# Strassen's scheme for 24 projection blocks of a three-block fp32 model, the sums on VectorE

## The chip, the cores and the metric

The kernel runs on one core of one Trainium2 chip. The metric is the device time of one execution in microseconds. Everything is fp32: a sequence of 512 tokens, model width 1024.

## The reference, cut to what matters

Three blocks follow each other on one activation matrix: a mixer of linear attention and sparse attention, a convolution and neighbourhood mixer with 16 experts, and two layers of a third kind. The change touches the projections of the third block and the store for weights of the experts.

```python
def even_layer(x, ...):
    proj = rms_norm_3(x, norm_g) @ w_in                # 1024 x 5632
    u_a, v_a, z_a, q_b, k_b, v_b, z_b = split_cols(proj, EVEN_SPLITS)
    a_out = chunked_sgu(u_a, v_a, ...) * silu(z_a)
    b_out = window_attention(q_b, k_b, v_b, sink) * silu(z_b)
    return concatenate([a_out, b_out]) @ w_out

def odd_layer(x, ...):
    proj = rms_norm_3(x, norm_g) @ w_in                # 1024 x 5 * 2048
    q, f_f, f_b, i, z = split_cols(proj, ODD_SPLITS)
    # f = lb + (1-lb) sigmoid(f_logit), k = 1-f, decays = exp(cumsum(log f)) in chunks of 64,
    # forward (f_f) and backward (f_b); o = both directions
    return (rms(o) * head_norm_g * silu(z)) @ w_out
```

## The kernel before, in words

Weights stream from HBM in blocks of 2 MB: 1024 rows by 512 columns, in SBUF as `w[128, 8, 512]`. `plan` lists them in the order of use, and `Chip.stream` issues their DMAs on SP's queue, each as soon as the slot it goes to is free (L202 to L212). Outside the experts four slots (`weight_ring`, `RING = 4`) turn over; in the experts stage eight do: the ring, three pairs of `work` slots and, last, `hT`.

`project` (L248) runs one list of tiles over the blocks. For a tile, TensorE accumulates one PSUM bank over eight 128-row pieces; a tile of kind "T" is 128 output columns by 512 tokens (L331), one of kind "N" has the tokens on the partitions (L335). Four tiles make a block. Tile n uses bank n mod R and waits until the eviction of tile n - R is done (R is 8 in the even layer's first projection, 4 in its second, 3 in the odd layer). ScalarE or VectorE evicts each tile in order of tiles. Behind tile n each engine runs whatever the dictionaries `tensor_beside`, `scalar_beside` and `vector_beside` hold for n; a key n - 0.5 is TensorE work in the middle of tile n. Each engine runs its part strictly in the written order, so a wait in it holds all that is behind it. A `project` is one block of the program, and the next starts when all engines have finished it.

The even layer (`even_layer`): six blocks (u, v, z, two each), then q, q and k/v with the gating (`even_gating`: layer norm on VectorE, a mix on TensorE that needs all of the norm, gates on VectorE) beside them, then the window attention.

The odd layer (`odd_group`) runs four head groups G. Each is one `project` with three banks: from the second group on eight tiles that add the group before to the residual (L2188), then the blocks F, B (forget gates of both directions), I, Q and Z, four tiles each, first tiles tF, tB, tI, tQ, tZ. Beside them: `log`, `scan`, `exponents`, `end_keys` for direction 0 during B and for direction 1 during I; `turn(d)` on TensorE needs `end_keys(d)`; `turn(1)` stands behind tile tI + 3; `products` and `step` run during Q, `gram`, `mask`, `output`, `norm_sum`, `root` and `finish` during Z.

`Norm` scales the activations into `hT` piece by piece on VectorE (L477, eight steps), once ScalarE has the reciprocal root; the first tile of a projection follows piece by piece.

Of the kernel before, what the change touches and what calls it, by code (L numbers as in the profile page):

```python
# [29 lines left out]
RING = 4  # L30
SLOT = 4096
# [79 lines left out]
class Chip:  # L111


    def __init__(self, nc, ctx, arrays, plan):
        self.nc, self.ctx, self.A, self.plan = nc, ctx, arrays, plan

        def sb(name, shape, dt=F32):
            return ctx.enter_context(nc.sbuf_tensor(name, shape, dt))

        self.xT = sb("xT", [P, KD, T])  # L120
        self.hT = sb("hT", [P, KD, T])
        self.ring = sb("weight_ring", [P, RING, SLOT])
# [12 lines left out]
        for n in ("tensor_step", "vector_step", "scalar_step", "pool_step", "aux_loaded", "tile_vector_done"):  # L135
# [6 lines left out]
        self.slot_of = [(i - first) % len(self.slots) if first <= i < first + 12 * E_ else i % RING  # L142
                        for i in range(len(plan))]
        self.arrived = {}
        self.issued = 0
        self.used = 0
# [66 lines left out]

    def block_view(self, i):
        _, kt, c = self.plan[i]
        return self.slots[self.slot_of[i]][:, 0:kt * c].rearrange("p (k c) -> p k c", k=kt)
# [29 lines left out]
def project(ch, nblocks, tiles, ahead=RING, extra_sync=None, vector_after=None, scalar_after=None,  # L246
# [19 lines left out]
    R = banks  # L266
    ready, by_act, by_dve = ch.counters("tile_ready", "tile_scalar_done", "tile_vector_done")
# [3 lines left out]
    def shape(t):  # L271
        b, kind, where, src, ntok, _ = t
        c = ch.plan[first + b][2] if b is not None else P
        if kind == "T":
            return min(P, c - where), ntok
        if kind == "N":
            return P, c
        if isinstance(kind, tuple):
            return P, kind[2] - kind[1]
        return P, P  # L280
# [5 lines left out]
    with nc.Block() as block:  # L286
# [7 lines left out]
        def _(pe):  # L294
            last = -1
            tensor_beside.get(-1, nothing)(pe)
            for n, t in enumerate(tiles):
# [21 lines left out]
                if kind == "M":  # L319
# [37 lines left out]
        @block.vector  # L357
        def _(dve):
            v = Line(dve, ch.S["vector_step"])
            if norm:  # L360
# [1362 lines left out]
def route(ch):  # L1723
# [80 lines left out]
def experts(ch):  # L1804
# [39 lines left out]
    with nc.Block() as block:  # L1844
        @block.sync
        def _(sp):
            ch.stream(sp, first + 12 * E_ + RING)
# [223 lines left out]
def even_gating(ch, beside, n0):  # L2071
# [18 lines left out]
    def layer_norm(line, dve):  # L2090
        for s in range(4):
# [4 lines left out]
        line.after(root, 1)  # L2096
        line(dve.reciprocal(mv[:, :, 1], mv[:, :, 1]))
        line.after(loaded, 16)
        for s in range(4):
            line(dve.tensor_scalar(v[:, s, :], v[:, s, :], mv[:, s, 0:1], mv[:, s, 1:2], SUB, MUL))  # L2100
            line(dve.tensor_tensor(v[:, s, :], v[:, s, :], gain, MUL))
            line(dve.tensor_tensor(v[:, s, :], v[:, s, :], shift, ADD), normed)

# [30 lines left out]
    beside.add(0, None, deviation, layer_norm)  # L2134
# [64 lines left out]

def even_layer(ch, norm):  # L2200
# [3 lines left out]
    for b in range(2):  # L2204
        tiles += [(b, "T", j * P, ch.hT, T, copy_to(u[:, 4 * b + j, :])) for j in range(4)]
    for b in range(2):
        tiles += [(2 + b, "N", s * P, ch.hT, T, copy_to(v[:, s, b * 512:(b + 1) * 512])) for s in range(4)]
    for b in range(2):
        tiles += [(4 + b, "T", j * P, ch.hT, T, act_to(z[:, 4 * b + j, :], ACT.Silu)) for j in range(4)]
    project(ch, 6, tiles, norm=norm)  # L2210
# [3 lines left out]
    for b in range(2):  # L2214
        tiles += [(b, "T", j * P, ch.hT, T, copy_to(q[:, 4 * b + j, :])) for j in range(4)]
# [3 lines left out]
    load = even_gating(ch, beside, 4)  # L2219
# [24 lines left out]
def odd_group(ch, G, norm):  # L2244
# [17 lines left out]
    by_dve, by_act = ch.S["tile_vector_done"], ch.S["tile_scalar_done"]  # L2262
    logged, scanned, decayed, ended = ch.counters("f_logged", "decay_scanned", "decay_exponents", "end_keys_ready")
# [8 lines left out]
    tF, tB, tI, tQ, tZ = [n0 + 4 * i for i in range(5)]  # L2272
    for d, dst in ((0, F), (1, B)):
        for j in range(4):
            lb = ch.sm[:, 16 * d + 4 * G + j:16 * d + 4 * G + j + 1]
            om = ch.sm[:, 32 + 16 * d + 4 * G + j:33 + 16 * d + 4 * G + j]

            def part_a(a, act, ps, sig, o=dst[:, j, :]):
                a(act.activation(o, ps, ACT.Sigmoid), sig)

            def part_v(v, dve, ps, sig, o=dst[:, j, :], k=kd[d][:, j, :], lb=lb, om=om):
                v(dve.tensor_scalar(o, o, om, lb, MUL, ADD))
                v(dve.tensor_scalar(k, o, -1.0, 1.0, MUL, ADD), sig)
            tiles.append((b0 + d, "T", j * P, ch.hT, T, (part_a, part_v)))
    tiles += [(b0 + 2, "N", s * P, ch.hT, T, copy_to(I[:, s, :])) for s in range(4)]
    for j in range(4):
        tmp = aT[j % 2].rearrange("p h v -> p (h v)")

        def q_a(a, act, ps, sig, j=j, tmp=tmp):
            if j >= 2:  # L2290
                a.after(by_dve, n0 + 7 + j)
# [6 lines left out]
    tiles += [(b0 + 4, "T", j * P, ch.hT, T, act_to(Z[:, j, :], ACT.Silu)) for j in range(4)]  # L2298

# [14 lines left out]
    def products(i):  # L2314
        def part(pe):
            for d in range(2):
                c = i if d == 0 else 7 - i
                s, rows = c // 2, slice(64 * (c % 2), 64 * (c % 2) + 64)
                if i == 0:
                    pe.wait_ge(natural.sem, natural.at(8))  # L2320
                else:
# [8 lines left out]
    def gram(h):  # L2330
        def part(pe):
            pe.wait_ge(by_dve.sem, by_dve.at(n0 + 9 + h))
# [43 lines left out]
    def log(d):  # L2376
        def part(a, act):
            a.after(by_dve, n0 + 4 * d + 4)
# [39 lines left out]
    def scan(d):  # L2418
        def part(v, dve):
            if d == 0:  # L2420
# [3 lines left out]
            for j in range(4):  # L2424
# [4 lines left out]
    def end_keys(d):  # L2429
        def part(v, dve):  # L2430
# [3 lines left out]
            v(dve.tensor_tensor(kd[d], kd[d], ed[d], MUL))  # L2434
            v(dve.tensor_tensor(ed[d].rearrange("p j (c t) -> p (j c) t", t=64),
# [31 lines left out]
    def finish(h):  # L2467
        def part(v, dve):
# [3 lines left out]
            v.after(by_act, 17 + h)  # L2472
            v(dve.scalar_tensor_tensor(Z[:, h, :], t, ch.v("hgrn_head_norm_g_3", 4 * G + h), Z[:, h, :], MUL, MUL))
        return part

    project(
        ch, b0 + 5, tiles, banks=3, norm=norm,
        tensor_beside={
            tI + 1: turn(0), tI + 3: turn(1), tQ: products(0), tQ + 0.5: products(1), tQ + 1: products(2),
            tQ + 1.5: products(3), tQ + 2: products(4), tQ + 2.5: products(5), tQ + 3: seq(products(6), gram(0)),  # L2480
            tZ - 0.5: gram(1), tZ: output(0), tZ + 0.5: seq(gram(2), output(1)), tZ + 1: seq(norm_sum(0), gram(3)),
            tZ + 1.5: seq(norm_sum(1), output(2)), tZ + 2: output(3), tZ + 2.5: seq(norm_sum(2), norm_sum(3))},
        scalar_beside={
            tB: log(0), tB + 2: exponents(0), tI: log(1), tI + 1: seq(exponents(1), to_natural(0)),
            tI + 3: to_natural(1), tZ: seq(square(0), square(1)), tZ + 1: seq(root(0), root(1), square(2)),
            tZ + 2: seq(square(3), last_roots)},
        vector_beside={
            tB + 1: scan(0), tB + 3: seq(end_keys(0), scan(1), end_keys(1)),
            tQ: seq(step(0), step(1)), tQ + 1: seq(step(2), step(3)), tQ + 2: seq(step(4), step(5)),
            tQ + 3: seq(step(6), *[mask(0), mask(1), mask(2), finish(0), mask(3), finish(1), finish(2), finish(3)])})  # L2490
# [116 lines left out]
```

## Time and profile before

| | us |
|---|---|
| median of 3 runs | 3687.27 (3686.51 to 3687.99) |
| profiled execution | 3687.83, of which the traced span 3686.1 |
| TensorE matmul busy | 3406.9 (92%) |
| TensorE weight load busy | 1654.7 (45%) |
| VectorE busy | 1217.0 (33%) |
| ScalarE busy | 733.1 (20%) |

Busy time of matmuls counts overlapped records once. A matmul of fp32 shows as two matmul records and two weight loads, so a tile of eight pieces has 16 of each. TensorE's granted clock is 0.967 of full speed over the span.

### The profile page before, as it was taken

The page shows a single profiled execution, that of the slowest core. Times are in us where ns is not written, and L with a number is a line of the kernel's source. Part 1 is how long each engine was busy: PE and PEld are TensorE (multiplying, and loading weights), DVE is VectorE, ACT ScalarE, POOL GpSimd, SP SyncE. Part 2 cuts the span into 40 slices and gives each one's busy share as a digit, 9 for nine tenths or more (in the row PEclk, how much of TensorE's full clock was granted, in tenths as well). Part 3 has the DMA queues.
Part 4 walks back from the last instruction along what each step waited for, and adds up shares of the span by engine and source line. Part 5 has one row for each costly group of instructions (what it writes and reads, how often), then busy time and mean ns, then how long its engine had stood idle before and what let it go on. Part 6 is the DMA issues. An engine that isn't in the chain of part 4 may idle for free. (4 is left out here: it accounts for less than half of the span.)

```text
span 3686.1 us, 36428 instructions
## 1 busy us (share of the span) xinstructions
PE 3406.9 (92%) x15170; PEld 1654.7 (45%) x15170; DVE 1217.0 (33%) x1973; ACT 733.1 (20%) x1128; POOL 0.2 (0%) x4
## 2 busy tenths in 40 slices
PE   7998998998999969989999987999999999999997
PEld 3485544443446533323233232445543544546454
DVE  3562238511466232221212212013432414233242
ACT  2110222302015220000000002011512223232223
POOL 0000000000000000000000000000000000000000
PEclk9997999999999979999999999999999999999999
DMA  7201042123110059999999998222111111111100
GB/s 261 78 3 69 23 154 104 46 89 129 69 61 26 23 210 428 428 427 428 428 428 427 428 427 341 69 86 73 46 69 46 69 46 69 46 69 46 69 23 23
DMA packets 120292, 588.13 MB, mean 160 GB/s; under 512 B 8896, under 2 KB 11072, under 8 KB 95424
## 3 DMA queue, kind: packets, MB, share of 16 engines
q1 hardware_dynamic: 120128, 585.80, 39.9%
q8 instruction: 121, 1.98, 0.2%
q14 instruction: 43, 0.35, 0.0%
HBM read 583.68 MB, written 2.10 MB: 159 GB/s over the span
## 5 line engine op out<-in xcount | busy, mean ns | idle before, releaser
L331 PE MATMUL ps<-hT,weight_ring 128*128 128x512 f32 x2624 | 1166.8, 601 | 42.8 <-DVE hT L477 13.4
L331 PEld LDWEIGHTS ps<-hT,weight_ring 128*128 128x128 f32 x2624 | 496.8, 192 | 645.2 <-issue 628.4
L331 PE MATMUL ps<-work,weight_ring 128*128 128x512 f32 (+1 forms) x960 | 425.1, 596 | 30.9 <-PEq L286 24.4
L331 PEld LDWEIGHTS ps<-work,weight_ring 128*128 128x128 f32 x960 | 184.0, 196 | 242.0 <-issue 233.6
L1891 PE MATMUL ps<-weight_ring,work 128*64 128x512 f32 x1024 | 236.0, 605 | 33.5 <-DMA weight_ring<-in_w_up 23.6
L335 PE MATMUL ps<-weight_ring,hT 128*128 128x512 f32 (+2 forms) x640 | 248.7, 544 | 0.0
L1891 PE MATMUL ps<-work 128*64 128x512 f32 x768 | 174.8, 597 | 23.6 <-DMA work<-in_w_up 12.4
L335 PEld LDWEIGHTS ps<-weight_ring,hT 128*128 128x128 f32 x640 | 117.7, 194 | 120.8 <-issue 118.8
L2020 DVE SCALAR_TENSOR_TENSOR xT<-ps,mod,xT 128x512 f32<-128x512 f32 x128 | 96.2, 751 | 226.4 <-PE ps L1909 224.0
L420 ACT COPY work<-ps 128x512 f32<-128x512 f32 (+1 forms) x85 | 48.2, 567 | 581.1 <-PE ps L335 290.9
L1891 PEld LDWEIGHTS ps<-weight_ring,work 128*64 128x64 f32 x1024 | 71.4, 138 | 189.9 <-issue 135.7
L1270 PE MATMUL ps<-work 64*128 64x256 f32 (+5 forms) x256 | 106.2, 522 | 20.1 <-DVE work L1314 13.1
L1945 PE MATMUL ps<-weight_ring,work 128*64 128x512 f32 x512 | 113.9, 596 | 2.6 <-issue 2.3
L1891 PEld LDWEIGHTS ps<-work 128*64 128x64 f32 x768 | 53.7, 136 | 137.3 <-issue 107.4
L2188 DVE TENSOR_TENSOR xT<-ps,xT 128x512 f32<-128x512 f32 x48 | 33.2, 692 | 202.6 <-PE ps L331 202.6
L1296 PE MATMUL ps<-work 128*64 128x128 f32 (+1 forms) x704 | 99.8, 285 | 0.0
L2015 DVE TENSOR_TENSOR work<-work,ps 128x512 f32<-128x512 f32 x32 | 33.9, 1059 | 196.7 <-PE ps L1891 196.1
L1971 ACT ACTIVATE work<-ps 128x512 f32<-128x512 f32 x32 | 19.1, 597 | 385.5 <-PE ps L1891 385.0
L2035 DVE COPY work<-ps 128x512 f32<-128x512 f32 x16 | 11.1, 692 | 244.3 <-PE ps L1945 244.3
L1580 DVE SCALAR_TENSOR_TENSOR work<-work,vectors 128x512 f32<-128x512 f32 x120 | 90.2, 752 | 4.3
L1945 PE MATMUL ps<-work 128*64 128x512 f32 x384 | 85.9, 596 | 3.5 <-issue 2.3
L1296 PEld LDWEIGHTS ps<-work 128*64 128x64 f32 (+1 forms) x704 | 81.6, 153 | 11.2 <-issue 10.2
(311 smaller groups left out, 3152.0 us busy)
## 6 DMA issues: line engine op xcount, KB each, us to landing
weight_ring<-in_w_gate SPq DMA_DIRECT2D x32, 2048.0 KB, 35.4
weight_ring<-in_w_down SPq DMA_DIRECT2D x32, 2048.0 KB, 35.4
weight_ring<-in_w_up SPq DMA_DIRECT2D x32, 2048.0 KB, 33.3
work<-in_w_up SPq DMA_DIRECT2D x24, 2048.0 KB, 32.0
work<-in_w_gate SPq DMA_DIRECT2D x24, 2048.0 KB, 35.4
work<-in_w_down SPq DMA_DIRECT2D x24, 2048.0 KB, 35.4
weight_ring<-in_w_in_odd SPq DMA_DIRECT2D x20, 2048.0 KB, 7.8
weight_ring<-in_w_in SPq DMA_DIRECT2D x18, 2048.0 KB, 9.0
```

The lines of the kernel that those rows point to most:

```text
L331: ins = pe.matmul(bank[0:m, 0:f], w[:, k, where:where + m], src[:, k, 0:ntok], start=k == 0, stop=k == kt - 1)
L335: ins = pe.matmul(bank[0:m, 0:f], src[:, k, where:where + P], w[:, k, c0:c0 + f], start=k == 0, stop=k == kt - 1)
L420: return (lambda a, act, ps, sig: a(act.copy(out, ps), sig), None)
L1270: ins = pe.matmul(self.score_banks(i)[:, c0:c0 + n], u["q"], k, start=True, stop=True)
L1296: ins = pe.matmul(self.ch.ps[u["rows"], self.value_bank + gi % 2, u["col"]:u["col"] + P], val, self.pT[(i - 3) % 2][:, t * P:(t + 1) * P], ...
L1580: v(dve.scalar_tensor_tensor(y[:, j, :], src, tap, y[:, j, :], MUL, ADD))
L1891: ins = pe.matmul(ps[64 * h:64 * h + 64, 1 + 2 * u + n, :], xs[:, 2 * (i % 2) + t, i // 2, :], w[:, t, c0:c0 + 512], start=i == 0 and t == ...
L1945: ins = pe.matmul(ps[64 * q:64 * q + 64, 7, :], hidT[:, i // 2, t, i % 2, :], w[:, t, q * 512:(q + 1) * 512], start=i == 0 and t == 0, sto ...
L1971: a(act.activation(sil[:, p, :], ps[:, 1 + p, :], ACT.Silu), silus)
L2015: v(dve.tensor_tensor(by_tile(hid[:, p, :]), strided(sil[:, p, :]), strided(ps[:, 3 + p, :]), MUL), hid_ready)
L2020: v(dve.scalar_tensor_tensor(ch.xT[:, n, :], ps[:, scatter_banks(e, i // 2)[i % 2], :], ch.mod2[:, 40 + n, 0:1], ch.xT[:, n, :], MUL, ADD) ...
L2188: v(dve.tensor_tensor(ch.xT[:, n, :], ps, ch.xT[:, n, :], ADD), sig)
```

## The change

A projection block of 1024 x 512 weights times 1024 x 512 activations is cut into halves on each side. Instead of four tiles (eight pieces of 512 columns each) it is computed as seven products of half size (Strassen's scheme in Winograd's form): each product is a tile of eight matmuls of 256 columns, two column halves of four pieces, in one bank. Four sums of weight quarters (`weight_sum`, 4 x 256 elements per partition each) and, once for each layer, four sums of activation quarters (`activation_sums`, the same size) are made on VectorE. The seven products are evicted by one ScalarE copy and seven VectorE additions of 128 x 512. This is done for u, v, z (six blocks) and q (two) of the even layer, and for F, B, I and Z of the four odd groups (sixteen). The sums of the next block stand behind early tiles of the current one; the first block of each layer has its sums ahead of the norm's scaling (`vector_first`), and the activation sums stand behind it.

What an eviction did on the way (sigmoid and the bounds for F and B, silu for z) is now done by quarters after the last addition to the quarter. In the odd layer the side work is spread anew over 7 tiles; `gated` is split from `finish`, `inner_keys` from `end_keys`. The third block's ring has three slots, since the fourth holds the activation sums; a new tensor `spare_slot` holds two or three of the weight sums there and is a ninth slot for weights in the experts stage, ahead of `hT` in the turn.

```diff
+RING3 = 3
+        self.spare = sb("spare_slot", [P, SLOT])
+        self.slots.insert(-1, self.spare[:, :])
+        self.slot_of = [i % RING if i < first else (i - first) % len(self.slots) if i < last else (i - last) % RING3
+                        for i in range(len(plan))]
...
+PRODUCTS = (1, 6, 7, 5, 3, 4, 2)
+def weight_sum(ch, i, n):
+        out, x, y, op = ((s1, a21, a22, ADD), (s2, s1, a11, SUB), (s3, a11, a21, SUB), (s4, a12, s2, SUB))[n]
+        v(dve.tensor_tensor(out, x, y, op), ch.S["weight_sums"])
+def activation_sums(ch):
+        for out, x, y in ((t1, b12, b11), (t2, b22, t1), (t3, b22, b12), (t4, t2, b21)):
+            v(dve.tensor_tensor(out, x, y, SUB), ch.S["h_sums"])
+    evictions = {1: (first, None), 6: (None, add((d12, d11, ADD), after_copy=True)), 7: (None, add((d21, d12, ADD))),
+                 5: (None, add((d22, d21, ADD), (d12, d12, ADD))), 3: (None, add((d12, d12, ADD))),
+                 4: (None, add((d21, d21, SUB))), 2: (None, add((d11, d11, ADD)))}
+    return {1: (a11, b11, 0, 0), 2: (a12, b21, 0, 0), 3: (s4, b22, 4, 0), 4: (a22, t4, 0, 4), 5: (s1, t1, 1, 1),
+            6: (s2, t2, 2, 2), 7: (s3, t3, 3, 3)}[p]
...
+                    for j in range(2):
+                        for k in range(4):
+                            ins = pe.matmul(bank[:, j * L:(j + 1) * L], st, mv, start=k == 0, stop=k == 3)
...
-            ch.stream(sp, ch.used + RING + 3)
+            ch.stream(sp, ch.used + RING + 4)
             sp.wait_ge(turned.sem, turned.at(9))
-            ch.stream(sp, ch.used + RING + 4)
+            ch.stream(sp, ch.used + RING + 5)
...
+    for s in range(4):
+        beside.add(s // 2, vector=variances(s))
+        beside.add(3 + 2 * s, vector=layer_norm(s))
+    load = even_gating(ch, beside, 10)
...
+    scalar = {
+        tB + 0: log(0), tB + 2: exponents(0), tI: log(1), tI + 2: seq(exponents(1), to_natural(0)),
+        tI + 5: to_natural(1), tZ + 1: square(0), tZ + 2: square(1), tZ + 3: root(0), tZ + 4: seq(root(1), square(2))}
+    vector = {
+        tB: bounded(0, (0, 1), 4), tB + 1: scan(0, (0, 1)), tB + 2: scan(0, (2, 3)), tB + 4: inner_keys(0),
+        tB + 5: end_keys(0), tI: bounded(1, (0, 1), 4), tI + 1: scan(1, (0, 1)), tI + 2: scan(1, (2, 3)),
+        tI + 3: inner_keys(1), tI + 4: end_keys(1), ...
+        tZ + 4: finish(1), tZ + 6: seq(gated(0), gated(1), finish(2), gated(2), finish(3), gated(3))}
+        tI + 2: turn(0), tI + 5: turn(1), ...
+        beside.add(t + 6, vector=bounded(d, (2, 3), 3))
+    for n, quarter in quarters_done(0):
+        beside.add(tZ + max(n, 5), scalar=open_gate(quarter, n))
+    beside.add(tZ + 6, scalar=last_roots)
+        beside.add(tB + 1 + n, vector=weight_sum(ch, first + 2, n))
+        beside.add(tI + min(4 + n, 6), vector=weight_sum(ch, first + 4, n))
```

## Rows read from the trace of the kernel before

**Rows 1.** Busy time by stretch; length, busy PE, PEld, DVE, ACT, POOL, clock, DMA
```profile
2304.00:2469.00 165.00, 164.68 (x381) 72.99 (x382) 5.44 (x8) 14.85 (x24) 0.00 (x0) 0.99 0.19 64
2981.60:3197.00 215.40, 209.76 (x745) 111.62 (x744) 70.77 (x94) 56.23 (x63) 0.00 (x0) 0.99 0.17 59
```
**Rows 2.** Timeline of TensorE in the even layer; columns: start, length, what
```profile
2507.26 7.03 PE L331 MATMUL ps<-hT,weight_ring 128*128 128x512 f32 x16
2514.12 1.05 PE L2116 MATMUL ps<-work 128*128 128x128 f32 x8
...
2546.05 3.62 PE L335 MATMUL ps<-weight_ring,hT 128*128 128x256 f32 x16
2549.51 1.05 PE L2116 MATMUL ps<-work 128*128 128x128 f32 x8
```
**Rows 3.** Weight loads grouped by line, even layer; busy, mean ns | idle before
```profile
L335 PEld LDWEIGHTS ps<-weight_ring,hT 128*128 128x128 f32 x64 | 11.9, 190 | 1.5
```
**Rows 4.** VectorE groups by line and shape, even layer and odd layer
```profile
L2093 DVE BATCH_NORM_STATS2 small<-work 128x6 f32<-128x512 f32 x8 | 5.6, 694 | 162.5 <-PEq L286 162.3
...
L2101 DVE TENSOR_TENSOR work<-work 128x1024 f32<-128x1024 f32 x4 | 4.9, 1226 | 0.1
...
L2100 DVE TENSOR_SCALAR work<-work,small 128x1024 f32<-128x1024 f32 x4 | 3.2, 812 | 1.1 <-DMA work<-in_gmlp 1.0
...
L2426 DVE TENSOR_TENSOR_SCAN work<-work 128x512 f32<-128x512 f32 x32 | 39.2, 1224 | 11.0 <-ACT work L2380 9.7 <-DVE work L2422 0.3
L2188 DVE TENSOR_TENSOR xT<-ps,xT 128x512 f32<-128x512 f32 x37 | 25.6, 692 | 142.4 <-PE ps L331 142.4
L2435 DVE TENSOR_TENSOR work<-work,small 128x2048 f32<-128x2048 f32 x8 | 18.3, 2292 | 0.3
L2282 DVE TENSOR_SCALAR work<-work,small 128x512 f32<-128x512 f32 x32 | 17.5, 546 | 172.3 <-ACT work L2279 172.2
...
L2283 DVE TENSOR_SCALAR work<-work 128x512 f32<-128x512 f32 x32 | 13.7, 427 | 1.1
```
**Rows 5.** Timeline of ScalarE: an activation of 2048 elements in an odd group
```profile
3079.86 1.91 ACT L2380 ACTIVATE work<-work 128x2048 f32<-128x2048 f32 x1
```
**Rows 6.** Timeline of TensorE, I block to Q block of that group
```profile
3084.58 1.91 PE L2308 MATMUL ps<-masks,work 128*128 128x128 f32 x16
3086.33 13.90 PE L335 MATMUL ps<-weight_ring,hT 128*128 128x512 f32 x32
```
**Rows 7.** Timeline from the end of one odd group to the next: TensorE, ScalarE, VectorE
```profile
3193.46 3.60 PE L331 MATMUL ps<-hT,weight_ring 128*128 128x512 f32 x8
3202.30 30.70 PE L331 MATMUL ps<-work,weight_ring 128*128 128x512 f32 x64 [5.25 <-PEq L286]
...
3193.70 1.28 ACT L2413 ACT_TABLE_LOAD   x1 [4.59 <-PE ps L2371]
...
3201.02 0.75 DVE L2473 SCALAR_TENSOR_TENSOR work<-work,vectors 128x512 f32<-128x512 f32 x1 [0.37 <-ACT work L424]
```
**Rows 8.** Busy time by stretch behind that gap (columns as in rows 1)
```profile
3204.00:3209.00 5.00, 5.00 (x8) 2.05 (x7) 0.00 (x0) 0.00 (x0) 0.00 (x0) 0.57 0.01 4
```
**Rows 9.** Timeline at the start of the even layer: ScalarE, VectorE, TensorE
```profile
2299.47 1.28 ACT L429 ACT_TABLE_LOAD   x1 [2.98 <-PEq L488]
...
2303.43 6.26 DVE L477 SCALAR_TENSOR_TENSOR hT<-xT,vectors,work 128x512 f32<-128x512 f32 x8 [8.12 <-ACT work L430]
...
2312.95 0.59 ACT L420 COPY work<-ps 128x512 f32<-128x512 f32 x1 [9.56 <-PE ps L331]
```
**Rows 10.** Busy time by stretch around the start of the experts and inside them
```profile
1350.00:1355.00 5.00, 3.13 (x14) 1.06 (x12) 2.04 (x5) 0.59 (x1) 0.00 (x0) 0.84 0.00 0
...
1600.00:1650.00 50.00, 46.37 (x210) 15.68 (x212) 11.74 (x19) 3.54 (x6) 0.00 (x0) 1.00 1.01 429
```
**Rows 11.** Timeline of SP's DMA issues: the first after the pause
```profile
1360.23 10.63 SPq L207 DMA_DIRECT2D weight_ring<-in_w_down  x4
```
**Rows 12.** Waits of TensorE from 1540 to 2300 us
```profile
PE ps L1891 <- DMA weight_ring<-in_w_up: 22.9, 25, 2.2
```

More of the change, by code:

```diff
@@ L266, in project @@
     R = banks
+    if ahead is None:
+        ahead = RING3 if first >= min(ch.sum_order) else RING
+    weight_ready, h_ready = ch.S["weight_sums"], ch.S["h_sums"]
     ready, by_act, by_dve = ch.counters("tile_ready", "tile_scalar_done", "tile_vector_done")
@@ L2088, in load, with variances, part @@
         loaded.total += 16
-    def layer_norm(line, dve):
-        for s in range(4):
+    def variances(s):
+        def part(line, dve):
             for i in range(2):
@@ L2095, in layer_norm, with part @@
                  var_ready if s == 3 else None)
[L2096 to L2099, printed above, removed]
+        return part
+    def layer_norm(s):
+        def part(line, dve):
+            if s == 0:
+                line.after(root, 1)
+                line(dve.reciprocal(mv[:, :, 1], mv[:, :, 1]))
+                line.after(loaded, 16)
             line(dve.tensor_scalar(v[:, s, :], v[:, s, :], mv[:, s, 0:1], mv[:, s, 1:2], SUB, MUL))
@@ L2197, in add_to_stream, with quarters_done, silu_quarter, part @@
     return norm
+def quarters_done(b):
+    return [(3, 3), (4, 1), (5, 2), (6, 0)]
+def silu_quarter(ch, x, done):
+    by_dve = ch.S["tile_vector_done"]
+    def part(a, act):
+        a.after(by_dve, done)
+        a(act.activation(x, x, ACT.Silu))
+    return part
 def even_layer(ch, norm):
@@ L2214, in even_layer @@
     for b in range(2):
-        tiles += [(b, "T", j * P, ch.hT, T, copy_to(q[:, 4 * b + j, :])) for j in range(4)]
+        seven_tiles(ch, tiles, b, False, quarters(q[:, 4 * b:4 * b + 4, :]))
     tiles += [(2, "T", j * P, ch.hT, T, copy_to(kv[:, j, :])) for j in range(2)]
@@ L2218, in even_layer @@
     beside = Beside()
[L2219 removed]
+    for n in range(4):
+        beside.add(1 + n, vector=weight_sum(ch, ch.used + 1, n))
+    load = even_gating(ch, beside, 10)
     beside.project(ch, 3, tiles, banks=4, extra_sync=load)
@@ L2271, in odd_group, with gates, part, bounded @@
     b0 = 1 if G else 0
[L2272 to L2281, printed above, removed]
-                v(dve.tensor_scalar(o, o, om, lb, MUL, ADD))
-                v(dve.tensor_scalar(k, o, -1.0, 1.0, MUL, ADD), sig)
-            tiles.append((b0 + d, "T", j * P, ch.hT, T, (part_a, part_v)))
-    tiles += [(b0 + 2, "N", s * P, ch.hT, T, copy_to(I[:, s, :])) for s in range(4)]
+    tF, tB, tI, tQ, tZ = n0, n0 + 7, n0 + 14, n0 + 21, n0 + 25
+    first = ch.used + b0
+    seven_tiles(ch, tiles, b0, False, quarters(F))
+    seven_tiles(ch, tiles, b0 + 1, False, quarters(B))
+    seven_tiles(ch, tiles, b0 + 2, True, quarters(I, True))
+    def gates(d, quarter, done):
+        def part(a, act):
+            x = quarters((F, B)[d])[quarter]
+            a.after(by_dve, n0 + 6 * d + done)
+            a(act.activation(x, x, ACT.Sigmoid), sigmoids)
+        return part
+    def bounded(d, rows, need):
+        def part(v, dve):
+            v.after(sigmoids, 4 * d + need)
+            for j in rows:
+                o, k = (F, B)[d][:, j, :], kd[d][:, j, :]
+                lb = ch.sm[:, 16 * d + 4 * G + j:16 * d + 4 * G + j + 1]
+                om = ch.sm[:, 32 + 16 * d + 4 * G + j:33 + 16 * d + 4 * G + j]
+                v(dve.tensor_scalar(o, o, om, lb, MUL, ADD))
+                v(dve.tensor_scalar(k, o, -1.0, 1.0, MUL, ADD), bounds)
+        return part
+    def open_gate(quarter, done):
+        def part(a, act):
+            x = quarters(Z)[quarter]
+            a.after(by_dve, n0 + 22 + done)
+            a(act.activation(x, x, ACT.Silu), gate_open)
+        return part
     for j in range(4):
@@ L2297, in odd_group @@
         tiles.append((b0 + 3, "T", j * P, ch.hT, T, (q_a, q_v)))
-    tiles += [(b0 + 4, "T", j * P, ch.hT, T, act_to(Z[:, j, :], ACT.Silu)) for j in range(4)]
+    seven_tiles(ch, tiles, b0 + 4, False, quarters(Z))
     def turn(d):
@@ L2423, in part @@
             v.after(logged, d + 1)
-            for j in range(4):
+            for j in rows:
                 x = F[:, j, :] if d == 0 else B[:, j, ::-1]
@@ new lines, in odd_group @@
+    for k, part in vector.items():
+        beside.add(k, vector=part)
+    for n in range(4):
+        if G:
+            beside.add(1 + n, vector=weight_sum(ch, first, n))
+        beside.add(tF + 1 + n, vector=weight_sum(ch, first + 1, n))
+        beside.add(tB + 1 + n, vector=weight_sum(ch, first + 2, n))
+        beside.add(tI + min(4 + n, 6), vector=weight_sum(ch, first + 4, n))
+    if norm:
+        ch.counter("h_sums")
+        beside.add(-1, vector=activation_sums(ch))
+    beside.project(ch, b0 + 5, tiles, banks=3, norm=norm, vector_first=weight_sums(ch, first) if norm else None)
```

157 lines of the change are left out of this document (119 added, 38 removed).

## The prediction, made before the change was run

> **What bounds the kernel now.** I read the page's busy shares first, then the busy time by stretch. TensorE is the bound: in the even layer's first projection it is busy 164.7 of 165.0 us, in an odd group 209.8 of 215.4, while VectorE works 5.4 and 70.8 us there [rows 1]. So a shorter TensorE stream pays at once, as long as VectorE keeps up. The exception is the experts stage: there the DMA engines are full at 429 GB/s and TensorE waits for weights in short pieces [rows 10, 12]. Third, I read the timelines of all engines through one odd group, because each engine runs in a written order and the chain logarithm, scan, exponents, keys, turn goes back and forth between them [rows 5, 6]. Last come the seams between program blocks, where TensorE is idle for 5.25 us [rows 7].
>
> **TensorE's work.** A tile of 16 records of 512 columns takes 2514.12 - 2507.26 = 6.86 us, one of 16 records of 256 columns 2549.51 - 2546.05 = 3.46 us [rows 2]: 429 and 216 ns a record. A block was 4 x 6.86 = 27.44 us and becomes 7 x 3.46 = 24.22. That is 3.22 us less, for 24 blocks **-77.3 us**. The doubled number of weight loads is hidden in that row: a load takes 190 ns [rows 3] and fits into the 216 ns pitch, with 26 ns to spare.
>
> Here a rule speaks against the change. The row shows loads on the same rows of the array as the running matmul, and a pitch no longer than the columns need. The Trainium skill, TensorE: Matmul & The Clock Gate, section "The mechanism", says that weight loads overlap with matmuls in flight only when the row group differs. By that rule a 256-column record would take 216 + 190 = 406 ns, a block 112 x 0.406 = 45.5 us; it is the last rival below. The pitch in rows 2 contradicts it.
>
> **VectorE's work for a block.** Four weight sums of 1024 elements at 1.226 us, seven PSUM additions at 0.692 us [rows 4], each with some 0.03 us between: 4 x 1.26 + 7 x 0.73 = 10.1 us against 24.2 of TensorE. In the even layer's first projection nothing else is there, and with eight banks it costs nothing. If that cover were gone, a block would wait up to 10 us.
>
> **Start of each layer (twice).** Before, VectorE began to scale at 2303.43, 4.0 us after ScalarE began the root [rows 9]. Four weight sums in front take 5.0 us: +1.0. Then the second product needs two activation sums behind all eight scalings: 6.26 + 2 x 1.26 = 8.8 us after the first scaling, while the first product (3.46, partly at the half clock) is done by about 6.2. Six products follow: the block ends 8.9 + 20.8 = 29.7 us after scaling began. Before, the first tile's eviction began 9.5 us after it [rows 9], so the tile ended at about 9.25, the block at 9.25 + 20.6 = 29.85. With the 1.0 the block is 0.85 later, where 3.22 earlier was booked: +4.1 each, **+8.2**.
>
> **Seam and gating in the even layer.** The last quarter's silu now follows a VectorE addition: +0.9. In the second projection VectorE has, up to the mix behind the eleventh tile, four variances (two statistics of 0.69 and an end of 0.2 each, 6.8 in all), 5.0 of sums, four norms of 0.81 + 2 x 1.23 (3.35 with gaps) and the additions [rows 4]; in the written order it is done at 38.9 us, TensorE is there at 38.1. +0.8. Together **+1.7**. These have one answer each within a microsecond.
>
> **An odd group, B and I.** I set VectorE's order against TensorE's tiles, time 0 at the end of F's last tile; an eviction can begin 0.27 us after a tile. The durations are those of the rows [rows 4, 5, 7]: 0.73 an addition, 1.04 a row of bounds (0.55 and 0.43 and their gaps), 1.25 a scan row, 1.26 a weight sum, 2.55 inner keys (a small copy and 2.29), 2.33 end keys, logarithm 1.28 (table) + 1.91, exponents 1.28 + 2 x 1.91 = 5.15.
> F's last addition ends at 1.0, its bounds at 3.1 and 5.2, the logarithm at 8.4. Then VectorE is full: ones for the scan and half of it to 11.1, sum 12.3, addition 13.1, scan 15.6, sum, two additions, sum, addition to 20.3; the exponents are there at 20.8; inner keys to 23.4, sum 24.6, addition 25.3, end keys 27.7, B's last addition 28.4 (its tile ended at 24.2: VectorE is 4 us late). B's bounds follow to 32.6, the logarithm to 35.8, scan, addition, scan to 41.6, exponents to 46.8, inner keys 49.4, addition 50.1, end keys **52.5**. TensorE reaches `turn(1)` after six I tiles and `turn(0)` (1.75, from 3084.58 to 3086.33 [rows 6]) at 24.2 + 20.8 + 1.75 = 46.7. So it waits 5.8 us where it had not waited: behind it on TensorE stand the last I product and all of Q. Four groups: **+23.2**. No tile waits for a bank: the nearest is tI + 1, which needs B's sixth addition at 25.3 and starts at 27.7.
>
> **The clock behind that wait.** After 5.25 us idle the granted clock was 0.57 in the stretch 3204 to 3209, and 64 records took 30.7 us instead of 64 x 0.429 = 27.5 [rows 7, 8]: 3.2 us lost. Bounds for a wait of 5.8 us: 0 and 3.2; I take 2.2, near the row, since the idle time is nearly the same, and below it, since this is the dearest of the three such seams. **+8.8**.
>
> **Q and Z.** Q is unchanged. In Z the same side work stands between seven shorter tiles; the nearest wait in my order is `output(2)` at 32.8 against `finish(0)` at 31.6: nothing. The end is new. Before, the roots of the last two heads ran during the last tile (from 3193.7) and the next group began 0.5 us after the last product of VectorE [rows 7]. Now they stand behind the last quarter's silu: addition to 0.9 us after the last tile, silu 1.5, two table loads and the first three activations 6.2, then VectorE's finish and gate for two heads, 4 x 0.74 = 3.0, and 0.5 for the seam: 9.7 us instead of 5.25. **+17.8** for four groups. The clock was low there already.
>
> **Experts.** DMA stands still at 1350 to 1355 since all slots are full [rows 10]; it goes on at 1360.23 with the first slot freed, and from there to the end of the experts it is the bound [rows 10 to 12]. With a ninth slot one more block of 2 MB is loaded in the pause, 2.1 MB / 0.427 = 4.9 us less to load afterwards: **-4.9**. Bounds: 0 if the last weights come as before, -4.9 if they come first. The shorter ring costs nothing: a load is due every 24 us and a transfer at full rate takes 4.9.
>
> **The sum.** -77.3 + 8.2 + 1.7 + 23.2 + 8.8 + 17.8 - 4.9 = -22.5 us. Made against the profiled execution (3687.83, 1.7 around its span), which lies 0.6 above the median of 3687.27: **3665**.
>
> **Rivals.**
> A. VectorE is not that late in I, or the clock stays up. My chain has some forty steps, and rows show each alone, not in this order. Without wait and clock loss it is -54.5 us, 3633; with half of both 3649. For it: VectorE is free for 6 of 24 us in F, and small gains at the start pass through. Against it: each duration is a row.
> B. VectorE is later than that. Three banks of half-size tiles give 10.4 us from a product to the need of its bank, where before it was 20.6. The margin is 2.4 us at tI + 1. If additions or sums on strided quarters took 10% longer, the two chains through B and I would end some 4 us later: 4 x 4 = +16, 3681; with a further bank wait it comes to no change.
> C. The ninth slot brings nothing (it does not do what it says): 3670.
> D. Slower than before: weight loads do not stay hidden when they fill 190 of 216 ns for a whole layer, with all other engines reading SBUF. The change has 24 x 112 = 2688 such records. The gain of 22.5 us is gone from 8.4 ns more a record (224 ns), and the kernel is slower by 0.2% from 227 ns. At 235 ns it is +29 us, 3716. Against it: 64 records of this shape keep to 216 ns in rows 2 and 3.
> E. The skill's rule on row groups holds: 24 x (45.5 - 27.4) is 434 us, 4120.
>
> **How the numbers follow.** The forecast has 0.48 (its own range 3655 to 3674, from the bounds of the clock and 1 us on each wait), A 0.20, B 0.20, C 0.05, D 0.06, E 0.01. The range is 3644 to 3683: it leaves out the far part of A (0.08), D, E, and the tail of B (0.03). About 0.2%, 7 us, is what a measurement of this kernel can tell from no change. Faster: 0.48 + 0.20 + 0.05 + 0.12 of B = 0.85. Same: 0.05 of B, 0.01 of D. Slower: 0.05 of D, 0.01 of E, 0.03 of B.
>
> **What would show it.** Right: 256-column records at 216 ns; TensorE idle some 6 us in each group until VectorE's end keys; the seam between groups at 9 to 10 us; a group still 213 to 217 us long, so that the odd layer gains almost nothing and the even layer 20 us; DMA still busy in 1330 to 1345. Wrong: no idle time ahead of the second turn (A), TensorE waiting for additions at its banks (B), a record above 220 ns (D).

## The result, and the profile after

The changed kernel takes 3668.4 us (median of 4 runs, 3666.4 to 3670.8) against 3687.6 of the kernel before on the same chip: a recorded ratio of 0.9944 with a 95% interval of 0.9931 to 0.9956 (the two medians alone give 0.9948). The profiled execution took 3666.36 us, which is 21.5 less than the profiled one of before; its span is 3664.5. The page's busy times, in us, with share and number of instructions:

```profile
PE 3336.9 (91%) x16322; PEld 1885.2 (51%) x16322; DVE 1459.9 (40%) x2245; ACT 714.9 (20%) x1104; POOL 0.2 (0%) x4
```

TensorE has lost 70 us of busy time, but the kernel only 21.5. The waits of TensorE from 2200 us on show the first part of the answer (who waited for whom: us in total, times, longest):

```profile
PE ps L452 <- PEq L392: 42.2, 6, 9.8
PE ps L2479 <- DVE work L2611: 23.9, 4, 6.0
PE ps L439 <- DVE hT L600: 15.6, 2, 9.4
...
PE ps L439 <- DVE weight_ring L292: 3.3, 2, 2.0
```

L2479 is `turn`, which waits for the end keys (L2611) four times for 6 us, where before it did not wait at all. The first line is the seams (PEq is TensorE's own sequencer, which starts the next block of the program): four of the six are 9.8 us, where rows 7 show 5.25.

One odd group on TensorE's timeline (start, length, what, idle before and its releaser), from the last I products to the next group:

```profile
2841.33 1.91 PE L2479 MATMUL ps<-masks,work 128*128 128x128 f32 x16
2843.08 3.62 PE L439 MATMUL ps<-spare_slot,weight_ring 128*128 128x256 f32 x16
2846.53 3.62 PE L439 MATMUL ps<-spare_slot,hT 128*128 128x256 f32 x16
2849.99 3.62 PE L439 MATMUL ps<-weight_ring 128*128 128x256 f32 x16
2859.57 3.58 PE L2479 MATMUL ps<-masks,work 128*128 128x128 f32 x16 [5.96 <-DVE work L2611]
2862.98 3.62 PE L439 MATMUL ps<-weight_ring,hT 128*128 128x256 f32 x16
...
2956.48 1.89 PE L439 MATMUL ps<-hT,weight_ring 128*128 128x256 f32 x8
2968.18 29.67 PE L452 MATMUL ps<-work,weight_ring 128*128 128x512 f32 x64 [9.81 <-PEq L392]
...
3183.21 29.67 PE L452 MATMUL ps<-work,weight_ring 128*128 128x512 f32 x64 [9.79 <-PEq L392]
```

Products start 3.45 us apart: 16 records of 256 columns at 216 ns, as in rows 2. `turn(0)` takes 1.75 us to the next start, `turn(1)` behind the wait 3.41: it ran at the lower clock. A whole group, from the first of the tiles that add a group's share to the residual (L452, `work`) to the next such tile, takes 3183.21 - 2968.18 = 215.03 us, where it took 215.41 (from 2986.89 to 3202.30, rows 7). Four of five blocks are cheaper by 27.44 - 24.17 = 3.27 us each there, and the group is 0.4 us shorter.

VectorE in the same stretch shows where the end keys come from, and that it is not simply full (lines in order of time):

```profile
2838.50 0.55 DVE L2448 TENSOR_SCALAR work<-work,small 128x512 f32<-128x512 f32 x1
2839.08 0.43 DVE L2449 TENSOR_SCALAR work<-work 128x512 f32<-128x512 f32 x1
2839.55 0.69 DVE L324 TENSOR_TENSOR work<-work,ps 128x512 f32<-128x512 f32 x1
2842.90 2.48 DVE L2598 TENSOR_TENSOR_SCAN work<-work 128x512 f32<-128x512 f32 x2 [2.67 <-ACT work L2552]
2845.42 0.69 DVE L324 TENSOR_TENSOR work<-work,ps 128x512 f32<-128x512 f32 x1
2846.14 2.48 DVE L2598 TENSOR_TENSOR_SCAN work<-work 128x512 f32<-128x512 f32 x2
2848.65 1.41 DVE L324 TENSOR_TENSOR work<-work,ps 128x512 f32<-128x512 f32 x2
2853.94 0.20 DVE L2604 COPY small<-work 128x32 f32<-128x32 f32 x1 [3.88 <-ACT work L2560]
2854.17 2.29 DVE L2606 TENSOR_TENSOR work<-work 128x2048 f32<-128x2048 f32 x1
2856.50 0.69 DVE L324 TENSOR_TENSOR work<-work,ps 128x512 f32<-128x512 f32 x1
2857.22 2.29 DVE L2611 TENSOR_TENSOR work<-work,small 128x2048 f32<-128x2048 f32 x1
```

Twice it waits for ScalarE (2.67 us for the logarithm, 3.88 for the exponents) while the chain goes through there.

The experts: the first slot is freed at 1358.90 (SP's next issue), and the last expert's scatter starts at 2267.86, which is 908.96 us later. Before these were 1360.23 [rows 11] and 2273.79: 913.56. The ninth slot brought 4.6 us, and the slot freed 1.3 us sooner the rest of the 5.9 us by which the scatter starts earlier.

### The profile page after: what moved, and what is told of

Read it like the earlier page. It is cut to its first block and busy times, and to the rows that moved or that the text cites. A ratio compares the mean times of both kernels' runs of the same rounds, so it can differ in the third digit from the quotient of the medians.

```text
span 3664.5 us, 39233 instructions
## 1 busy us (share of the span) xinstructions
PE 3336.9 (91%) x16322; PEld 1885.2 (51%) x16322; DVE 1459.9 (40%) x2245; ACT 714.9 (20%) x1104; POOL 0.2 (0%) x4
## 5 line engine op out<-in xcount | busy, mean ns | idle before, releaser
L452 PE MATMUL ps<-hT,weight_ring 128*128 128x512 f32 x1472 | 663.0, 606 | 28.2 <-ACT hT L591 8.8
L452 PE MATMUL ps<-work,weight_ring 128*128 128x512 f32 (+1 forms) x960 | 425.3, 596 | 49.2 <-PEq L392 42.6
L452 PEld LDWEIGHTS ps<-hT,weight_ring 128*128 128x128 f32 x1472 | 279.9, 194 | 368.6 <-issue 354.0
L452 PEld LDWEIGHTS ps<-work,weight_ring 128*128 128x128 f32 x960 | 184.4, 196 | 259.0 <-issue 250.6
L2014 PE MATMUL ps<-weight_ring,work 128*64 128x512 f32 x944 | 214.3, 597 | 32.8 <-DMA weight_ring<-in_w_up 18.7
L324 DVE TENSOR_TENSOR work<-work,ps 128x512 f32<-128x512 f32 x168 | 115.5, 687 | 272.9 <-PE ps L439 270.3
L2014 PE MATMUL ps<-work 128*64 128x512 f32 x688 | 156.5, 597 | 21.4 <-DMA work<-in_w_up 13.3
L439 PE MATMUL ps<-weight_ring 128*128 128x256 f32 x768 | 174.0, 380 | 0.0
L439 PEld LDWEIGHTS ps<-weight_ring 128*128 128x128 f32 x768 | 145.2, 190 | 19.4
L439 PE MATMUL ps<-hT,weight_ring 128*128 128x256 f32 x576 | 137.2, 394 | 17.6 <-DVE hT L600 15.6
L439 PE MATMUL ps<-weight_ring,spare_slot 128*128 128x256 f32 x576 | 132.3, 383 | 3.3 <-DVE weight_ring L292 3.3
L439 PEld LDWEIGHTS ps<-hT,weight_ring 128*128 128x128 f32 x576 | 113.2, 198 | 39.1 <-issue 22.9
L439 PEld LDWEIGHTS ps<-weight_ring,spare_slot 128*128 128x128 f32 x576 | 109.8, 192 | 19.0 <-issue 4.1
L2138 DVE TENSOR_TENSOR work<-work,ps 128x512 f32<-128x512 f32 x32 | 33.9, 1060 | 192.0 <-PE ps L2014 191.4
L2068 PE MATMUL ps<-weight_ring,work 128*64 128x512 f32 x448 | 100.2, 595 | 4.0 <-DMA weight_ring<-in_w_down 2.4
```

Source lines behind the costliest of these rows:

```text
L324: v(dve.tensor_tensor(out, x, got, op), sig if out is steps[-1][0] else None)
L439: ins = pe.matmul(bank[:, j * L:(j + 1) * L], st, mv, start=k == 0, stop=k == 3)
L452: ins = pe.matmul(bank[0:m, 0:f], w[:, k, where:where + m], src[:, k, 0:ntok], start=k == 0, stop=k == kt - 1)
L2014: ins = pe.matmul(ps[64 * h:64 * h + 64, 1 + 2 * u + n, :], xs[:, 2 * (i % 2) + t, i // 2, :], w[:, t, c0:c0 + 512], start=i == 0 and t == ...
L2068: ins = pe.matmul(ps[64 * q:64 * q + 64, 7, :], hidT[:, i // 2, t, i % 2, :], w[:, t, q * 512:(q + 1) * 512], start=i == 0 and t == 0, sto ...
L2138: v(dve.tensor_tensor(by_tile(hid[:, p, :]), strided(sil[:, p, :]), strided(ps[:, 3 + p, :]), MUL), hid_ready)
```

## The experiments

Executions differ upstream of the change: in the kernels with nine slots the first slot is freed between 1356.3 and 1363.9 us, with the same code up to there. On the second chip the kernel before spread from 3679 to 3695 us. So beside each time I give one distance in the trace, **D**: from the start of the last expert's scatter to the start of the first tile behind the last odd group. TensorE's rows for it, first of the kernel before, then of the changed one:

```profile
2273.79 3.95 PE L1909 MATMUL ps<-work 64*128 64x512 f32 x16 [0.86 <-DVE work L2035]
...
3635.20 8.70 PE L331 MATMUL ps<-work,weight_ring 128*128 128x512 f32 x16 [5.22 <-PEq L286]
```

```profile
2267.86 3.95 PE L2032 MATMUL ps<-work 64*128 64x512 f32 x16 [0.86 <-DVE work L2158]
...
3613.31 9.06 PE L452 MATMUL ps<-work,weight_ring 128*128 128x512 f32 x16 [9.81 <-PEq L392]
```

It is 1361.4 us before and 1345.5 in the changed kernel. Each D is read from one execution, and it too moves by 2 to 3 us with the clock between executions of the same code (the run with eight slots shows it), so a difference of D is safe only where the places that moved are named.

### Which part brings what

**Only the slots.** Both layers as before; ninth slot and ring of three kept.

```diff
# in short: these functions are exchanged whole
-def even_gating, even_layer, odd_group   # of the changed kernel
+def even_gating, even_layer, odd_group   # of the kernel before
```

> Even and odd layer as before (four tiles a block, no sums); of the change only the ninth slot in the experts stage and the ring of three stay. Theory (the ninth slot is worth 4.9 us, the shorter ring nothing): 3681.6 us against 3686.5 of before, and the last expert's scatter begins 909 us after the first slot is freed instead of 913.6. Rival (the ring of three costs something in the third block): above 3684 us, with waits of TensorE for weights of the third block. The distance from here to the run with only the odd layer as before is the worth of the eight even blocks; by the terms of the sum it is 77.3 / 3 = 25.8 less 4.1, 1.7 and two clock losses of 1.8 each, 16 us.

Measured: 3685.3 us against 3688.3 in the same session (ratio 0.9990, 0.9979 to 1.0). The scatter begins 2265.08 - 1356.27 = 908.8 us after the first free slot, 4.8 less than before, and D is 1361.7. The ninth slot brings its 4.8 us. The shorter ring costs nothing that shows in the third block: D is within 0.3 us of before, and TensorE has no wait for weights there. The median shows 3.0 us less, which this spread (3678.6 to 3688.9 in ten executions) can't tell from 4.8; by the time alone (above 3684) the rival would have looked right.

**Eight slots.** The changed kernel without the ninth.

```diff
-        self.slots.insert(-1, self.spare[:, :])
...
-            ch.stream(sp, ch.used + RING + 4)
+            ch.stream(sp, ch.used + RING + 3)
...
-            ch.stream(sp, ch.used + RING + 5)
+            ch.stream(sp, ch.used + RING + 4)
```

> The changed kernel with eight slots in the experts stage as before (spare_slot holds only weight sums). Theory (the DMA-bound stage begins with one block more to load, 2.1 MB at 427 GB/s): 4.9 us slower than the changed kernel, 3673. Rival (the 6.3 us between the two traces were all the ninth slot): 6 us or more slower. Second rival (nothing: another limit ends the stage): within 1 us.

Measured: 3669.9 us, only 1.5 above the changed kernel. The experts do take 2273.21 - 1359.04 = 914.2 us instead of 909.0, 5.2 more. Half of it came back behind them: D is 3616.20 - 2273.21 = 1343.0, 2.5 less than in the changed kernel, though this part of the code is the same. Three tiles behind short idle times ran at the full clock in this execution and at the lower one in the changed kernel, 1.7 us each: two behind seams, and the second product of the odd layer. About half of that was lost again, where other tiles (the first turn above all, 2.8 us lost for 1.7) stayed at the lower clock for longer. By the time alone this would have been a miss for the ninth slot.

**The odd layer as before**, even layer changed.

```diff
# in short: this function is exchanged whole
-def odd_group   # of the changed kernel
+def odd_group   # of the kernel before
```

> The changed kernel with the whole odd layer as before (four tiles a block, no sums), the even layer and the ninth slot as changed. Theory (16 of the 24 blocks bring nothing, since the wait, the clock and the longer seam take what the products save): from the first odd matmul to the last group's end 836.5 us instead of 837.0, and 1 us less at its start: 3666 us, within 3 us of the changed kernel. Rival (the products in the odd layer bring a part, the gain in the even layer is smaller than read): 5 us or more slower than the changed kernel.

Measured: 3665.2 us, D = 3611.43 - 2265.74 = 1345.7. Against the run with only the slots (1361.7) the eight even blocks bring 16.0 us, as worked out. Of the two clock losses of 1.8 us in that working one stands at a seam with 2.06 us of idle time that the kernel before has too; it ran at the lower clock here and at the full one in the run with only the slots, so that this loss is luck, and without it the even blocks bring some 17.7 us. Against the changed kernel (1345.5) the **sixteen odd blocks bring 0.2 us**. In this pair both seams of the even layer ran at the same clock. The 0.2 stands for nothing measurable, not for a gain: the medians, 3665.2 and 3668.4 from different sessions, even put the kernel with the odd layer as before ahead.

### What eats the odd layer's products

**`turn(1)` later.**

```diff
-        tI + 2: turn(0), tI + 5: turn(1), tQ: products(0), ...
+        tI + 2: turn(0), tQ - 0.5: turn(1), tQ: products(0), ...
```

> The changed kernel with one move: turn(1) on TensorE stands in the middle of the first Q tile instead of behind the sixth I product. Theory (TensorE waits 5.96 us in each odd group for VectorE's end keys and then runs 1.7 us slower at the lower clock): both go, the seventh I product and half a Q tile (3.45 + 3.43 us) lie in front of the wait, 4 x 7.6 = 30 us less, 3638 us against 3668. Rival A (the wait only moves: products(0) behind the Q tile then waits for the copies of the turned keys): TensorE shows a new wait of 3 to 6 us at L2497 and the gain is under 15 us. Rival B (the clock loss is not from this wait): the wait goes, 24 us less, and some record group still shows the half clock.

Measured: 3638.8 us (ratio to before 0.9871, 0.9857 to 0.9886), D = 1316.6, that is 28.8 less than the changed kernel. TensorE's timeline:

```profile
2855.80 3.62 PE L439 MATMUL ps<-weight_ring,hT 128*128 128x256 f32 x16
2859.70 3.67 PE L452 MATMUL ps<-hT,weight_ring 128*128 128x512 f32 x8 [0.28 <-DVE work L324]
2863.21 1.91 PE L2479 MATMUL ps<-masks,work 128*128 128x128 f32 x16
2864.95 3.60 PE L452 MATMUL ps<-hT,weight_ring 128*128 128x512 f32 x8
2868.48 1.71 PE L2497 MATMUL ps<-work 64*128 64x128 f32 x16
```

`turn(1)` doesn't wait and takes 1.74 us; the copies of the turned keys are done when `products(0)` (L2497) comes, so rival A falls. A bank wait of 0.28 us is new. Both losses, the wait and the clock behind it, came from this one place; the four groups bring 28.8 / 4 = 7.2 us each, where 7.6 was worked out.

**Small sums beside B.** What is the wait made of? This kernel leaves out nearly all of block I's four weight sums (it sums one column in 256), so its block I is not the true one.

```diff
+        if small:
+            out, x, y = out[:, :, 0:1], x[:, :, 0:1], y[:, :, 0:1]
...
-        beside.add(tB + 1 + n, vector=weight_sum(ch, first + 2, n))
+        beside.add(tB + 1 + n, vector=weight_sum(ch, first + 2, n, small=True))
```

> Leaves out most of the four weight sums of block I beside block B (one column in 256 is summed, the instruction stays), so block I's products are not the true ones. It tells what the wait at turn(1) is made of. Theory (a serial chain of ScalarE and VectorE that is longer than seven... six short tiles, with VectorE's load only part of it): worked out with VectorE free of 4 x 1.1 us in B, the end keys come at 49.7 instead of 52.5 us after F's end, so the wait falls from 5.96 to about 3.0 us, not to 0. Rival (VectorE's load in B is all of it): the wait falls below 1.5 us. Second rival (load plays no part): it stays at 5.5 to 6 us.

Measured, in a single execution: 3667.5 us. The wait fell from 5.96 to 3.86 us:

```profile
2847.46 3.62 PE L441 MATMUL ps<-spare_slot,weight_ring 128*128 128x256 f32 x16
2850.92 3.62 PE L441 MATMUL ps<-spare_slot,hT 128*128 128x256 f32 x16
2854.37 3.62 PE L441 MATMUL ps<-weight_ring 128*128 128x256 f32 x16
2861.84 3.67 PE L2481 MATMUL ps<-masks,work 128*128 128x128 f32 x16 [3.86 <-DVE work L2613]
2865.31 4.59 PE L441 MATMUL ps<-weight_ring,hT 128*128 128x256 f32 x16
2869.74 0.59 PE L454 MATMUL ps<-hT,weight_ring 128*128 128x512 f32 x1
```

Both rivals fall: a third of the wait is the load of these sums on VectorE. Two thirds are left without it: the serial chain through two engines, with the other work of VectorE that stands in it, is still longer than six half-size tiles. The keys came 50.6 us after F's end where I had worked out 49.7; I did not follow these 0.9 us up. The time hides the gain, since the first slot was freed 5.0 us later here than in the changed kernel: D is 3614.57 - 2272.87 = 1341.7, 3.8 us less, where the four waits together are 8.5 shorter (15.4 for 23.9). The rest went to the clock. In the group shown the turn took 3.47 us to the next start and the product behind it 4.43 instead of 3.45, so that 2.7 us were lost instead of 1.7. It is not shown that the shorter wait caused this: over its four groups this run lost 2.7, 3.0, 3.0 and 1.4 us behind 3.86 us of idle time, and the run with eight slots, with the full wait of 5.96, lost 2.8, 1.9, 1.7 and 1.7.

**Z with four tiles**, on top of the late turn.

```diff
-    seven_tiles(ch, tiles, b0 + 4, False, quarters(Z))
+    tiles += [(b0 + 4, "T", j * P, ch.hT, T, act_to(Z[:, j, :], ACT.Silu)) for j in range(4)]
...
-        tZ + 4: seq(norm_sum(1), output(2)), tZ + 5: output(3), tZ + 5.5: seq(norm_sum(2), norm_sum(3))}
+        tZ + 1.5: seq(norm_sum(1), output(2)), tZ + 2: output(3), tZ + 2.5: seq(norm_sum(2), norm_sum(3))}
```

> The kernel with turn(1) moved into the first Q tile, and in it block Z of the odd groups as before (four tiles, silu at the eviction, roots under the last tile). Theory (Z's seven products give 3.3 us a group and take 4.6 at the seam): 4 x 1.3 = 5 us faster than with seven products, 3634 us, seam 5.25 us instead of 9.8. Rival (the longer seam is hidden or has another cause): slower by 13 us, 3652.

Measured: 3630.0 us, 8.8 less than with seven products; D = 1308.6, 8.1 less. The seam is back at 5.24 us:

```profile
2955.41 30.25 PE L452 MATMUL ps<-work,weight_ring 128*128 128x512 f32 x64 [5.24 <-PEq L392]
```

So in this order Z's seven products cost more than they gave. Of the 8.1 us 5.2 are the price that I worked out, 4 x (9.81 - 5.24 - 3.27). Another 1.7 and 1.6 are luck of the clock: the seam with 2.05 us of idle time and the second product of the odd layer ran at the full clock in this execution, and at the lower one in that of the late turn alone. The seams between groups lost 0.5 more.

### A better order

**Start and seam of the even layer**, on top of the late turn (Z with seven products).

```diff
-    beside.add(-1, vector=activation_sums(ch))
+    beside.add(-1, vector=first_sums(ch, first))    # T1, T2, S3, T3, S4, T4
...
-    vector_first=weight_sums(ch, first)
+    vector_first=early_sums(ch, first)              # S1, S2
...
-            for n, quarter in quarters_done(b):
+            for n, quarter in quarters_done(b)[:4 if b == 4 else 3]:
...
+    beside.add(0, scalar=lambda a, act: a(act.activation(rest, rest, ACT.Silu)))
```

> The kernel with turn(1) moved, and two more moves: only two of the four weight sums stand in front of the norm's scaling at a layer's start, the other two behind it in turn with the activation sums; and the last silu of z (even layer) stands behind the seam. Theory: the start of scaling comes 1.0 us earlier in both layers, the seam is 0.65 shorter (1.98 to 1.3 us idle), and the first product behind it runs at the full clock, 1.7: 1.0 + 1.0 + 0.65 + 1.7 = 4.4 us faster than with turn(1) alone, 3634. Rival (the low clock behind a short idle time does not hang on its length): 2.6 us faster or less, and the first product still takes 5.2 us.

Measured: 3632.8 us, 6.0 less than with the late turn alone; D = 1310.0, 6.6 less.

```profile
2451.54 3.69 PE L446 MATMUL ps<-hT,weight_ring 128*128 128x256 f32 x16 [1.32 <-PEq L399]
```

The seam is 1.32 us, and the product behind it runs at the full clock (5.38 before the move). It did so in both runs with this seam; with the longer one (1.98 us) it did in one run of six. Worked out were 4.4 us. By the luck told below 1.7 more came at the next seam and 1.6 at the second product of the odd layer; 0.7 was lost at the seams between the groups, and waits for banks took 0.3 more.

**Z's side work one product earlier**, on top of that.

```diff
-        tZ: gram(1), tZ + 1: output(0), tZ + 2: seq(gram(2), output(1)), tZ + 3: seq(norm_sum(0), gram(3)),
-        tZ + 4: seq(norm_sum(1), output(2)), tZ + 5: output(3), tZ + 5.5: seq(norm_sum(2), norm_sum(3))}
+        tZ: gram(1), tZ + 1: output(0), tZ + 2: seq(norm_sum(0), gram(2), output(1)),
+        tZ + 3: seq(norm_sum(1), gram(3), output(2)), tZ + 4: output(3), tZ + 5: seq(norm_sum(2), norm_sum(3))}
...
+    beside.add(tZ + 5, scalar=last_roots)
+    beside.add(tZ + 6, scalar=open_gate(*quarters_done(0)[3][::-1]))
```

> The kernel of the run before, and in block Z the norm sums, outputs and roots stand one product earlier; the roots of the last two heads on ScalarE stand ahead of the last quarter's silu instead of behind it. Theory (the seam is the chain norm sum, four table loads and activations, finish and gate, of which one product of 3.45 us more now covers a part): the seam falls from 9.8 to about 7.4 us, 4 x 2.4 = 10 us faster, 3624. Rival (the earlier order makes TensorE wait for roots or masks inside Z): new waits of TensorE at the outputs, as long or longer than what the seam gains.

Measured: **3619.0 us** (ratio to before 0.9807, 0.9788 to 0.9825), D = 1296.8.

```profile
2940.64 1.88 PE L2552 MATMUL ps<-work,masks 128*128 128x512 f32 x4
2942.36 3.62 PE L446 MATMUL ps<-hT,weight_ring 128*128 128x256 f32 x16
2952.45 17.77 PE L459 MATMUL ps<-work,weight_ring 128*128 128x512 f32 x37 [6.48 <-PEq L399]
```

A whole product lies between the last norm sums (L2552) and the seam, where it was half of one, and the seam falls to 6.48 us; four times 3.3 us is the gain of 13. The half product is 1.7 of the 3.3; ScalarE's roots ahead of the last silu were changed in the same run, and the two were not tried apart. Worked out were 2.4 us a seam, so the size was a miss. No new wait stands in Z. With this order Z's seven products are worth having: a group gains 3.27 us by them and its seam is 6.48 - 5.24 = 1.24 longer than with four tiles, which makes 8 us for four groups. The whole D is 11.8 us below that with four tiles; the rest is the moves at the starts and the even seam (4.3) and the clock, for and against. (Four tiles with the new order of Z were not tried.) This kernel beats both, with every product of the change kept.

## Why the prediction came out right, point by point

- **The sum.** Forecast -22.5 us against the profiled execution; measured -21.5. The likeliest case held, and no rival: `turn(1)` waits (against A), no bank wait in B and I (B), the ninth slot loads one block more in the pause (C), the products at the full clock keep to 216 ns a record (D, E). So the rule of the Trainium skill, TensorE: Matmul & The Clock Gate, section "The mechanism", that weight loads overlap with matmuls in flight only when the row group differs, does not hold for these matmuls: by it the starts would be 6.5 us apart, an estimate from rows 2 and 3 (16 x 0.406), and they are 3.45.
- **TensorE's work.** Forecast 24.22 us a block, measured 7 x 3.453 = 24.17: -78.5 instead of -77.3.
- **Start of each layer.** The even one came to the tenth: scaling begins at 2299.53, the block ends at 2329.25, 29.7 us later. In the odd one the second product, behind 2.02 us of idle time, ran at the lower clock, which the sum did not have. VectorE and TensorE there:

```profile
2775.38 6.26 DVE L600 SCALAR_TENSOR_TENSOR hT<-xT,vectors,work 128x512 f32<-128x512 f32 x8
...
2776.28 6.01 PE L439 MATMUL ps<-hT,weight_ring 128*128 128x256 f32 x16 [9.37 <-DVE hT L600]
2784.32 5.38 PE L439 MATMUL ps<-weight_ring,spare_slot 128*128 128x256 f32 x16 [2.02 <-DVE weight_ring L292]
2789.53 3.62 PE L439 MATMUL ps<-weight_ring 128*128 128x256 f32 x16
```

  The second product takes 5.21 us to the next start instead of 3.45: +1.8. The clock had come back before it and fell again: the granted clock in the middle and at the end of the first product, and in the second (columns as in rows 1):

```profile
2780.00:2781.00 1.00, 1.00 (x4) 0.82 (x3) 0.93 (x3) 0.00 (x0) 0.00 (x0) 0.50 0.00 0
2781.00:2782.30 1.30, 1.30 (x6) 0.78 (x5) 1.26 (x2) 0.00 (x0) 0.00 (x0) 1.00 0.00 0
...
2784.00:2789.50 5.50, 5.18 (x16) 4.29 (x17) 2.62 (x3) 0.00 (x0) 0.00 (x0) 0.69 0.00 0
```

- **Seam and gating.** Forecast +0.9 and +0.8; measured 1.98 - 1.16 = 0.8 and a wait of 0.9 at the mix. Missed: the product behind the seam ran at the lower clock.

```profile
2452.26 5.38 PE L439 MATMUL ps<-hT,weight_ring 128*128 128x256 f32 x16 [1.98 <-PEq L392]
2457.48 3.62 PE L439 MATMUL ps<-weight_ring,spare_slot 128*128 128x256 f32 x16
```

  The term was right in its place and 1.8 us too small. With it, and with the luck taken out, the even blocks bring 17.7 us and not the 20 that the prediction gives as a sign.
- **The wait at `turn(1)`.** Forecast 5.8, measured 5.96. What made this work was to write VectorE's order out against TensorE's tiles; busy shares (VectorE at 40%) show nothing of it.
- **The clock behind it.** Forecast 2.2, measured 3.41 - 1.75 = 1.7 in each of four groups of this execution. It is no fixed price: the run with eight slots, the same code here, lost 1.7 to 2.8.
- **The odd seam.** Forecast 9.7, measured 9.8.
- **Experts.** Forecast -4.9, measured -4.6 to -5.2 in three pairs of traces. The first slot was freed 1.3 us earlier beside, which is luck: with the same code up to there it is freed up to 3.7 us later than in the kernel before and up to 4.0 us earlier.

The misses (1.8 + 1.8 at short idle times, against 2.1 too much at the long waits, 1.2 in the products and 1.3 of luck) nearly cancel: by them alone it would be -23.5. Of the 2.0 us left, 0.9 is the clock behind an idle time of 5.77 us ahead of the even layer, which is there before too (1.9 us lost for 1.0), and the rest some tenths each in the wait (+0.6), the odd seam (+0.4) and the experts (+0.3). That the total came within 1 us is luck, since the clock alone moves it by 2 to 3; that it came near is not, as each of the dear terms (products, wait, odd seam, experts) is within some 6% of its size, the clock apart.

## What to carry to other kernels

When tiles get shorter, every chain that was hidden behind a fixed number of tiles must be measured again in microseconds: here six tiles of 3.45 us and a turn no longer cover a chain of 28 us through two other engines, and one tile no longer covers the roots at the end. Write the order of the second busiest engine out against the tiles before the change, as its mean load hides the wait; and if a wait appears, move the consumer before you lighten the producer: one moved key was worth 29 us, leaving out a block's sums on VectorE, a third of the wait, 4 us. A part of a change can be worth nothing in one order (sixteen blocks, 0.2 us) and some 45 us in another: D is 1345.7 with the odd layer as before and 1296.8 with the last order, of which 3.4 us belong to the moves in the even layer.

## What the runs showed of the hardware

A short idle time costs TensorE its clock in one execution and not in another, with the same code and the same idle time. Behind the even seam the changed kernel idled 1.98 us and its first product took 5.22 us to the next start. In the run with eight slots the idle time is the same and the product takes 3.5:

```profile
2458.09 3.69 PE L438 MATMUL ps<-hT,weight_ring 128*128 128x256 f32 x16 [1.98 <-PEq L391]
```

At the next seam 2.06 us of idle time are followed by 15.67 us for 32 records in the kernel before and in the changed one, and by 13.97 in four of the runs. The granted clock of the changed kernel ahead of the even seam and behind it (stretch, length, busy time of PE, PEld, DVE, ACT and POOL, clock, DMA):

```profile
2447.00:2452.00 5.00, 3.28 (x16) 2.54 (x14) 1.31 (x2) 1.26 (x2) 0.00 (x0) 1.00 0.12 19
2452.00:2457.00 5.00, 4.74 (x14) 3.92 (x15) 3.19 (x6) 0.00 (x0) 0.00 (x0) 0.66 1.01 370
```

0.66 is a mix of the two levels, 1.2 and 2.4 GHz. Over the third block of all ten traces, idle times up to 1.75 us were never followed by it, those of 3.85 us and more always. Between these the length did not decide: of 19 idle times of 1.98 to 2.12 us, 14 were followed by the lower clock and five not, and of five of 2.52 to 2.94 us, all ahead of the second product of a layer, none. What does decide stays open. So each place with an idle time near 2 us carries 1.7 us that come and go between executions.

The longer idle times have a spread too. The four seams of 5.25 us in the kernel before lost 1.6, 3.1, 2.1 and 1.7 us; the prediction took its bound of 3.2 from the dearest. A change of 5 us should be read from a distance in the trace that holds only the part it touches, as D here, and where 2 us matter D is to be read place by place too.
